# One item instead of four for the narrow branch of a three-branch attention

## The reference, cut to what matters

```python
n_cmp = (T - CMP_BLOCK) // CMP_STRIDE + 1                      # 31
valid = block_end[None, :] <= np.arange(T)[:, None]
s = jnp.einsum('bgrtd,bgnd->bgrtn', q, kc) * d ** -0.5
p = jax.nn.softmax(jnp.where(valid, s, NEG), axis=-1)
p = jnp.where(valid, p, 0.0)
o_cmp = jnp.einsum('bgrtn,bgnd->bgrtd', p, vc)
...
o_nsa = gates[0] * o_cmp + gates[1] * o_slc + gates[2] * o_win
y_nsa = o_nsa * jax.nn.silu(ng)
```

## Time and profile before

| | us |
|---|---|
| median of 3 runs (lowest, highest) | 3102.16 (3097.86, 3105.52) |
| the profiled execution: time, span | 3101.18, 3099.4 |
| the phase that is changed, in the span | about 2004.2 to 2203.0 |

### The profile page before, as it was taken

How to read it: one execution, slowest core, us unless ns; L and a number is a source line. 1 busy time by engine, 2 the same in 40 slices (tenths; PEclk the granted TensorE clock), 3 DMA queues, 4 the chain that set the end, 5 groups by cost and what they waited for, 6 DMA issues and landing times. The chain is left out here.

```text
span 3099.4 us, 35532 instructions
## 1 busy us (share of the span) xinstructions
PE 2867.2 (93%) x14186; PEld 2254.8 (73%) x14186; DVE 1079.5 (35%) x1761; ACT 1020.5 (33%) x1493; POOL 1180.8 (38%) x396
## 2 busy tenths in 40 slices
PE   8999999999889998889999799778899989999998
PEld 6887788887689677668878587255687736778876
DVE  2110215997434542241110401556503335621103
ACT  3331232233544424342221321244323435332212
POOL 4444453444363256254444441111242211554443
PEclk9999999999999999989999899888899989999999
DMA  4222232233200323122222223200222110222221
GB/s 156 97 101 88 82 121 81 95 137 127 89 1 2 143 88 123 41 82 95 95 95 95 82 95 151 77 28 14 102 95 96 55 51 31 79 95 95 96 94 68
DMA packets 41574, 266.50 MB, mean 86 GB/s; under 512 B 4208, under 2 KB 5616, under 8 KB 13168
## 3 DMA queue, kind: packets, MB, share of 16 engines
q1 hardware_dynamic: 37856, 256.47, 22.6%
q10 hardware_dynamic: 3600, 8.39, 0.7%
HBM read 248.07 MB, written 16.78 MB: 85 GB/s over the span
## 5 line engine op out<-in xcount | busy, mean ns | idle before, releaser
L210 POOL TENSOR_TENSOR weights_lo<-weights_raw,weights_hi 128x2048 fp32r<-128x2048 f32 x196 | 918.4, 4686 | 1561.8 <-ACT weights_hi L199 1561.8
L240 PE MATMUL psum<-x_hi,weights_hi 128*128 128x512 f32 (+1 forms) x2368 | 938.7, 396 | 80.9 <-DVE x_lo L360 35.4
L241 PE MATMUL psum<-x_lo,weights_hi 128*128 128x512 f32 (+1 forms) x2368 | 927.2, 392 | 0.0
L242 PE MATMUL psum<-x_hi,weights_lo 128*128 128x512 f32 (+1 forms) x2368 | 927.0, 391 | 0.0
L199 ACT ACTIVATE weights_hi<-weights_raw 128x2048 fp32r<-128x2048 f32 x202 | 386.6, 1914 | 784.3 <-PE psum L242 703.8
L240 PEld LDWEIGHTS psum<-x_hi,weights_hi 128*128 128x128 f32 x2368 | 453.6, 192 | 199.1 <-issue 84.6
L242 PEld LDWEIGHTS psum<-x_hi,weights_lo 128*128 128x128 f32 x2368 | 452.8, 191 | 94.3
L241 PEld LDWEIGHTS psum<-x_lo,weights_hi 128*128 128x128 f32 x2368 | 454.2, 192 | 90.0 <-issue 0.2
L416 DVE SCALAR_TENSOR_TENSOR arena<-arena,psum 128x512 f32<-128x512 f32 x66 | 45.4, 687 | 567.3 <-PE psum L242 567.3
L240 PE MATMUL psum<-h_hi,weights_hi 128*128 (+1 forms) x528 | 207.7, 393 | 7.3 <-PEq L381 7.3
L241 PE MATMUL psum<-h_lo,weights_hi 128*128 (+1 forms) x528 | 206.0, 390 | 0.0
(11 more groups left out here) (324 smaller groups left out, 3395.6 us busy)
## 6 DMA issues: line engine op xcount, KB each, us to landing
weights_raw<-in_stream SPq DMA_DIRECT2D x202, 1024.0 KB, 4.8
keep_gates<-arena ACTq DMA_DIRECT2D x24, 256.0 KB, 2.0
arena<-keep_gates SPq DMA_DIRECT2D x3, 2048.0 KB, 9.6
arena<-keep_x SPq DMA_DIRECT2D x3, 2048.0 KB, 8.4
keep_x<-arena SPq DMA_DIRECT2D x2, 2048.0 KB, 9.8
arena<-in_w_k SPq DMA_DIRECT2D x2, 2048.0 KB, 8.4
arena<-in_na_bias SPq DMA_DIRECT2D x1, 3584.0 KB, 12.4
arena<-in_x_t SPq DMA_DIRECT2D x2, 1024.0 KB, 8.0
```

The lines of the kernel that those rows point to most:

```text
L210: K.nc.gpsimd.tensor_tensor(K.wlo[:, 1 - slot, :, :], K.raw[:, 1 - slot, :, :], K.whi[:, 1 - slot, :, :].bitcast(F32), ALU.subtract).then_ ...
L240: K.nc.tensor.matmul(out, whi, xhi, start=start, stop=False)
L241: K.nc.tensor.matmul(out, whi, xlo, start=False, stop=False)
L242: return K.nc.tensor.matmul(out, wlo, xhi, start=False, stop=stop)
```

## The change

The compressed branch becomes one item for each pair of heads, marked "whole", with all four tiles of queries in it. Its (c, None, 0) stands ahead of the eight other items of its pair, so the list is 4 x (1 + 8) = 36 items long. In a whole item

- `scores` issues eight matmuls of 31 columns into two banks (124 columns in each), `turn` eight transposes;
- `before` is three instructions on 248 elements: bias, negated maximum for each of the eight rows, and the addition of that maximum (broadcast);
- `exponential` is one instruction, without bias and without accumulator;
- `after` is five: sums of the eight rows, the second mask over 248 elements, reciprocal, gate, and the multiplication of all 248 by their eight factors;
- `copy` takes both banks whole (31 x 1024) into buffers of their own (units 24 or 26 of the arena), and there is no `product`: the two matmuls a tile are issued at the head of the product of the selected branch of each tile.

The pieces of the fill stand at (9p)//4 in place of (11p)//4. The other two attentions keep their order.

```diff
-    items = [(c, i, b) for c in range(len(pairs)) for i in range(NT) for b in range(len(pairs[c]["branches"]))]
+    items = []
+    for c in range(len(pairs)):
+        branches = range(len(pairs[c]["branches"]))
+        at_once = [b for b in branches if pairs[c]["branches"][b].get("whole")]
+        items += [(c, None, b) for b in at_once] + [(c, i, b) for i in range(NT) for b in branches if b not in at_once]
...
+    def is_whole(x):
+        return items[x][1] is None
+
+    def first_of(x):
+        return items[x][1] == 0 and (x == 0 or items[x - 1][1] is None or items[x - 1][0] != items[x][0])
+
+    def products(x):
+        return sum(not is_whole(y) for y in range(x + 1))
+
+    def wide(x):
+        return NT * 2 * br(x)["width"](0)
+
+    def eight(at, x):
+        return K.small[:, at + 8 * (items[x][0] % 2):at + 8 * (items[x][0] % 2) + 8]
+
+    def rows_of_eight(ap, x):
+        return ap.rearrange("p (u n) -> p u n", n=br(x)["width"](0))
+
+    def by_side(ap, x):
+        return ap.rearrange("p s (i n) -> p s i n", i=NT)
+
+    def scored(x):
+        return K.ps[:, scores_bank(x):scores_bank(x) + 2, :wide(x) // 2]
+
+    def weighted(x):
+        return prob(x)[:, 0, :wide(x)].rearrange("p (s n) -> p s n", s=2)
...
+                if is_whole(x):
+                    out = by_side(scored(x), x)
+                    for i in range(NT):
+                        for side in range(2):
+                            q, k = br(x)["scores"](i, side)
+                            last = nc.tensor.matmul(out[:, side, i, :], q, k, start=True, stop=True)
+                    last.then_inc(s("att_scores").sem, s("att_scores").n())
+                    return
...
+                if is_whole(x):
+                    p = rows_of_eight(prob(x)[:, 0, :wide(x)], x)
+                    for i in range(NT):
+                        for side in range(2):
+                            last = nc.tensor.transpose(K.ps[:p.shape[2], 4 + side, P * i:P * i + P], p[:, NT * side + i, :], K.mat("ident"))
+                    last.then_inc(s("att_turned").sem, s("att_turned").n())
+                    return
...
+                if is_whole(x):
+                    return
...
+                opens = b == min(range(len(pairs[c]["branches"])), key=lambda u: (bool(pairs[c]["branches"][u].get("whole")), u))
+                alone = not any(branch.get("whole") for branch in pairs[c]["branches"])
+                if opens and not alone:
+                    at, branch = whole_units[c % 2], [u for u in pairs[c]["branches"] if u.get("whole")][0]
+                    for side, rows in enumerate(SIDES):
+                        nc.tensor.matmul(K.ps[rows, out_bank(c), P * i:P * i + P], branch["v"](0, side),
+                                         A[:branch["width"](0), at + side, P * i:P * i + P], start=True, stop=False)
...
+                if is_whole(x):
+                    step, out, peak = s("att_bias"), by_side(scored(x), x), eight(WMAX, x).rearrange("p (s i) -> p s i", s=2)
+                    nc.vector.tensor_tensor(out, out, br(x)["bias"], ALU.add).then_inc(step.sem, step.n())
+                    dve.wait_ge(step.sem, step.base + step.pending)
+                    nc.vector.tensor_reduce(peak, out, AX.X, ALU.max, negate=True).then_inc(step.sem, step.n())
+                    dve.wait_ge(step.sem, step.base + step.pending)
+                    low = peak.unsqueeze(3).broadcast_to([P, 2, NT, br(x)["width"](0)])
+                    nc.vector.tensor_tensor(out, out, low, ALU.add).then_inc(
+                        s("att_max").sem, s("att_max").n())
+                    return
...
+                if is_whole(x):
+                    p, r, w = prob(x)[:, 0, :wide(x)], eight(WRSUM, x), br(x)["width"](0)
+
+                    def then(ins):
+                        ins.then_inc(step.sem, step.n())
+                        dve.wait_ge(step.sem, step.base + step.pending)
+                    then(nc.vector.tensor_reduce(eight(WSUM, x), rows_of_eight(p, x), AX.X, ALU.add))
+                    then(nc.vector.tensor_tensor(by_side(weighted(x), x), by_side(weighted(x), x), br(x)["mask"], ALU.mult))
+                    then(nc.vector.reciprocal(r, eight(WSUM, x)))
+                    pair = r.rearrange("p (s i) -> p s i", s=2)
+                    then(nc.vector.tensor_tensor(pair, pair, br(x)["gate"], ALU.mult))
+                    nc.vector.tensor_tensor(rows_of_eight(p, x), rows_of_eight(p, x), r.unsqueeze(2).broadcast_to([P, 2 * NT, w]),
+                                            ALU.mult).then_inc(s("att_prob").sem, s("att_prob").n())
+                    return
...
+                if is_whole(x):
+                    nc.scalar.activation(weighted(x), scored(x), ACT.Exp).then_inc(
+                        s("att_exp").sem, s("att_exp").n())
+                    return
...
+                act.wait_ge(s("att_turned").sem, s("att_turned").at(x + 1))
+                if x >= 2 and products(x - 2):
+                    act.wait_ge(s("att_pv").sem, s("att_pv").at(products(x - 2)))
+                if is_whole(x):
+                    w = br(x)["width"](0)
+                    nc.scalar.activation(turned(x)[:w], K.ps[:w, 4:6, :], ACT.Copy).then_inc(s("att_copied").sem, s("att_copied").n())
+                    return
...
+    def each_tile(at):
+        return masks[:, at:at + 32 * NT].rearrange("p (i n) -> p i n", n=32)[:, :, :N_CMP].unsqueeze(1).broadcast_to([P, 2, NT, N_CMP])
+
+    def tile_gates(c):
+        return K.small[:, GATE:GATE + 24 * NT].rearrange("p (i n) -> p n i", n=24)[:, c:c + 5:4, :]
...
-            "width": lambda i: N_CMP, "gate": gate(0, c),
-            "bias": lambda i: (slice(0, N_CMP), both(masks[:, 32 * i:32 * i + N_CMP])),
-            "mask": lambda i: masks[:, 128 + 32 * i:128 + 32 * i + N_CMP],
+            "width": lambda i: N_CMP, "gate": tile_gates(c), "whole": True, "bias": each_tile(0), "mask": each_tile(128),
...
-    slots = [((11 * p) // 4, 2) for p in range(16)]
+    slots = [((9 * p) // 4, 2) for p in range(16)]
     phase_attention_pairs(K, "nsa", pairs, (A, 16), (A, [48, 50]), load,
-                          fill=FillTiles(K, "gates_2", slots, take_gate, make_silu), x_back=True)
+                          fill=FillTiles(K, "gates_2", slots, take_gate, make_silu), x_back=True, whole_units=[24, 26])
```

26 lines of the change are left out of this document (14 added, 12 removed).

## The result

| | before | after |
|---|---|---|
| median, us (lowest, highest; 4 runs each on one chip) | 3101.10 (3097.86, 3105.52) | 3058.06 (3056.65, 3059.86) |
| ratio, 95% interval | | 0.986 (0.9848 to 0.9873) |
| span of the profiled execution | 3099.4 | 3054.9 |
| start of the next phase's first VectorE instruction, in the span | 2203.27 | 2161.23 |

The change makes the kernel 43 us faster. I had forecast 14, with a range from 3075 to 3099; so the sign was right and the size was off by a factor of three. The trace puts 42.0 us into the changed phase. Ahead of it each stretch has its old length within 1 us; behind it lie 2.5 us of the 44.5 by which the two spans differ.

What follows compares the result with a forecast made beforehand. The serial VectorE-ScalarE chain plus 27.2 us of score waits was taken to bound the phase. Removing 32.0 us and adding 14.6 saves 17.4; 80% of it, 13.9, gives 3101.2 - 13.9 = 3087.3 us, range 3075 to 3099.

Steps and rivals of the forecast that it cites:

- What bounds the phase: Changed phase: the serial chain of VectorE and ScalarE, plus 27.2 us of VectorE's score waits and a little at both ends.
- The whole item: VectorE and ScalarE chain: one whole item takes 3.65 us, so the four added ones take 14.6 us.
- If the score waits stay what they are, all of it does ... I take 80%: Share of the chain's 17.4 us saving that arrives: 59% if both latenesses shrink, all if score waits stay; 80% taken, 13.9 us.
- Their place moves: PE: matmul counts stay, only their place moves, with fill pieces every 2.25 items in place of every 2.75; no time priced.
- two shares of the 17.4 us: Chain's saving, 32.0 us removed less 14.6 added; either 59% of it arrives, 10.3 us, or all of it.
- 1.7 us for each of 16 pieces: VectorE's 27.2 us of score waits read as arising wherever the next item's scores stand behind a piece of the fill.
- 16 compressed items at 2.00 us: VectorE and ScalarE chain: removing the compressed items takes away 32.0 us.
- GpSimd's four halts: VectorE instructions held while GpSimd makes a weight tile's low part: 12.8 us in all, expected to remain unchanged.
- A: PE with less slack runs fill pieces at the lower clock, score waits rise 10.2 us to 37.4: 3094.0 us; chance 0.22.
- D: The order of the fill, not the chain, sets the phase's time, so the kernel stays at 3101 us; chance 0.04.
- C: PE waits longer once per pair and its clock falls; at 0.65 the phase is 17 us longer, 3118; chance 0.05.
- B: PE waits less and its clock holds, so half the score waits go too, 13.6 us: 3070.2 us; chance 0.14.
- the chain's bound of 22.2: Largest chain saving, if each wide operation costs only 0.225 us and a whole item 2.45 us: 3079.0 us.

Runs made afterwards that it cites:

- b_slots9: The kernel before with only the fill's slots changed, (9p)//4 in place of (11p)//4, all 48 items kept: 3083.47 us, ratio 0.9937.
- b_warm: The kernel before with PE repeating an item's scores while it waits to turn them, where no piece of the fill stands in front: 3094.92 us, ratio 0.9967.
- b_s9_warm: The kernel before with slots (9p)//4 and PE repeating scores while it waits: 3081.73 us, ratio 0.9933.
- a_shift1: The changed kernel with each piece of the fill one item later and the silu one item after the taking instead of two: 3053.95 us, ratio 0.9843.
- a_gate1: The changed kernel with only the silu moved, one item after the taking in place of two: 3063.43 us, ratio 0.9874.
- s_both: a_shift1 with GpSimd's low part in four instructions and ScalarE's weight split in two halves, in each phase with such a fill: 3100.29 us, ratio 0.9992.

## Why the prediction was wrong, point by point

**What bounds the phase: right.** VectorE and ScalarE form a serial chain, and PE's lateness comes on top. The account of VectorE above closes to 1.3 us.

**The whole item: right in its own time.** 3.53 us against 3.65. Its operations of 248 elements took 0.41 to 0.42 us (0.425 taken), and the exponential 0.38 (0.47 taken, from a row of 256 elements that has an accumulator read behind it).

**The step that failed, in its largest part:** "If the score waits stay what they are, all of it does ... I take 80%". The forecast held the 27.2 us of the earlier trace rows for fixed; they fell by 16.0. Behind it stands the sentence on PE, "Their place moves" with pieces that come every 2.25 items, which I left without a price. b_slots9 measures it: 21 us by the median, 17.7 in the trace (16.2 without the masks). I had even written what made it, that behind a piece there "stood up to now a compressed item, 2.00 us of chain, which PE's lateness outlasted", and used it only to choose between two shares of the 17.4 us. The count that was missing is short: for each piece, which two items VectorE has in hand. It gives 11 places of 16 before and none after, and 17.3 of the 27.2 us stood at them; it says where to look, and not how much there is to gain. The reading "1.7 us for each of 16 pieces" was wrong as well: 6.3 us stood behind no piece, and with a quarter of the fill 12.0 us were left.

**A term that was mis-sized:** 16 compressed items at 2.00 us. They cost 2.75 (trace) to 3.1 us (median), since PE's turn and scores do not always fit under a compressed item even without fill (2.7 us at 2130.63, at the lower clock, against 1.9). I read an item's price from VectorE's rows alone; it is the longer of the two engines' steps. Whole items cost 4.3 to 5.4 in place of 3.65. Together 22 to 28 us in place of 17.4.

**The two together:** 21.3 (slots) + 25.4 (from b_slots9, 3083.5, to 3058.1) = 46.7 against a before of 3104.8, and 43.0 against the 3101.1 of the changed kernel's own group; these differ only by the two medians of before. With each kernel against its own before, the second part is 43.0 - 21.3 = 21.7. b_slots9 being the step between the two kernels, the parts must add up to the whole; what is measured is their sizes, and only in this order, for the old slots reach to item 41 and do not exist in 36 items.

**The waits foretold:** exponentials 36, measured 34.2; right. Scores 24 to 32, measured 11.2; wrong. PE ahead of its transposes 30, measured 17.2; wrong; I put it down to the same cause, which was not tried for these waits. Phase 185, measured 157. GpSimd's four halts: 10.4 us in the 32 gate multiplications (15.6 - 32 x 0.16, below), in place of 12.8; they stayed, less 2.4 us.

```profile
L2141 DVE TENSOR_TENSOR small<-small 128x2 f32<-128x2 f32 x32 | 15.6, 486 | 1.1
```

**The rivals.** A (PE takes the gain back, 3094.0) and D (no gain) are ruled out by the result; C (the clock falls) too, since it rose. A's price of a piece at the lower clock was too high besides: 2.34 us from two starts, where the whole piece of the earlier trace rows took 1.9 more than that of the earlier trace rows. B came nearest, with half of the score waits gone (they lost 59%), though 3058 is under its 3066 too, and it named the clock as the reason. The clock did rise, though to 0.90 and not over the 0.92 I had asked for. b_warm prices that reason: 10 us for a clock of 0.89. b_s9_warm shows that little of it adds to the slots. So B had the right place and a small part of the cause; that it came nearest is in part luck. The Trainium skill's rule that denser matmuls keep the clock up ("TensorE: Matmul & The Clock Gate", section "HAM oscillation") agrees with b_warm, 0.84 to 0.89. Here the price was small, because only a late PE pays for a slow clock.

**Why the range missed:** its lower end was 3101 less 26, from the chain's bound of 22.2 and a little of B. No term in it let the score waits go by their place. Had I bounded "moved at nothing" as I bounded each duration, the bound would have been the 27.2 us themselves, and 3101.2 - 17.4 - 27.2 = 3056.6 would have stood in the range.

**What stays open:** why the score waits of a_shift1 are 9.1 us less than those of a_gate1; why a place with a compressed item in hand costs half as much in b_slots9 as before; and the waits of the changed kernel behind pieces that have long items in front of them.

## What to carry to other kernels

Where one engine looks ahead by a fixed number of items, price an item at the longer of its own chain and of what the other engine must do meanwhile, and for each piece of independent work write down which items the waiting engine has in hand; a change of the list of items changes both. A wait that you read off the old trace is not a constant of the new one: bound it from zero to its full size. An edit to a class that several phases use is tried in one phase at a time, since s_both gained 8 us in one and lost 57 in the next. And when a third engine halts the one that bounds, the halts are summed over all its groups of instructions before a gain is put down to anything else.
